# Hyena's filters and their spectra computed inside RWKV's preparation stage; the shift by a token as a product with a constant matrix

## The reference, cut to what matters

```python
# RWKV: mix with the two neighbours, per segment (256 context rows, 1024 latent rows)
x = u + mu * (0.5 * (u_before + u_behind) - u)        # zero beyond the ends of a segment
# then per token: kk = k * w_kk, normed per head; w, a = sigmoid(base + tanh(..) @ lora); k per direction

def hyena_filters(length, w1, b1, f1, w2, b2, f2, w3):
    ...
    hid = jnp.sin(f1 * (z @ w1 + b1))
    hid = jnp.sin(f2 * (hid @ w2 + b2))
    h = (hid @ w3).reshape(length, HY_ORDER, 2, HY_W)
    return (h * jnp.exp(-t * deltas)[:, None, None, :]).astype(F32)
# two_sided_fftconv multiplies the spectrum of the input by the spectrum of (h_f, h_b), for two orders
```

## Time and profile before

| | us |
|---|---|
| median of 3 runs (5839.44 to 5861.69) | 5848.86 |
| the profiled execution: time / span | 5849.2 / 5847.6 |
| PE busy in the span | 4508.9 (77%) |
| DVE busy | 2637.6 (45%) |
| ACT busy | 1397.6 (24%) |
| POOL busy | 650.7 (11%) |
| mean granted TensorE clock, share of full speed | 0.863 |

### The profile page before, as it was taken

One profiled execution on the slowest core, in us unless ns is written; L12 is line 12 of the kernel. 1 busy time (PEld: TensorE's weight loads), 2 busy tenths in 40 slices (PEclk: granted clock), 3 DMA queues, 4 the chain that ended last, 5 costly groups with the idle time before them and its releaser, 6 DMA issues. The chain is left out here.

```text
span 5847.6 us, 71599 instructions
## 1 busy us (share of the span) xinstructions
PE 4508.9 (77%) x26346; PEld 3697.1 (63%) x26346; DVE 2637.6 (45%) x4928; ACT 1397.6 (24%) x2564; POOL 650.7 (11%) x640
## 2 busy tenths in 40 slices
PE   6999987677998991899552169995489966876877
PEld 4998874455887881899552048885379952333555
DVE  3567743453332005211265766764533543323654
ACT  3233214432221002111022323332331100001333
POOL 1111111110000001000012221111112410110001
PEclk8999996688999995899865579997699976888998
DMA  4444422231112102221204543332434523343004
GB/s 153 161 143 139 136 97 104 83 112 58 47 47 61 54 18 102 92 96 56 90 23 164 197 123 99 99 95 66 133 118 131 190 95 137 140 156 121 7 7 151
DMA packets 433801, 599.74 MB, mean 103 GB/s; under 512 B 187209, under 2 KB 326065, under 8 KB 427331
## 3 DMA queue, kind: packets, MB, share of 16 engines
q1 hardware_dynamic: 377721, 443.54, 24.0%
q0 software_dynamic: 39824, 147.45, 6.5%
q10 hardware_dynamic: 16000, 5.30, 0.4%
HBM read 425.95 MB, written 170.25 MB: 102 GB/s over the span
## 5 line engine op out<-in xcount | busy, mean ns | idle before, releaser
L336 PE MATMUL g_in_g_acc<-g_in_g_whi,g_in_hi 128*128 128x444 f32 (+4 forms) x960 | 357.2, 372 | 15.2 <-DVE g_in_g_wlo L326 9.9
L337 PE MATMUL g_in_g_acc<-g_in_g_wlo,g_in_hi 128*128 128x444 f32 (+4 forms) x960 | 346.3, 361 | 0.0
L338 PE MATMUL g_in_g_acc<-g_in_g_whi,g_in_lo 128*128 128x444 f32 (+4 forms) x960 | 346.1, 360 | 0.0
L212 PE MATMUL g_even_acc<-g_even_w_hi,h_hi 128*128 128x384 f32 (+1 forms) x960 | 317.1, 330 | 30.6 <-DVE g_even_w_lo L254 30.6
L212 PE MATMUL g_down_acc<-g_down_w_buf,fT 128*128 128x256 f32 x1408 | 306.0, 381 | 16.5 <-DMA g_down_w_buf<-in_w_down 16.5
L214 PE MATMUL g_even_acc<-g_even_w_lo,h_hi 128*128 128x384 f32 (+1 forms) x960 | 316.9, 330 | 0.0
L215 PE MATMUL g_even_acc<-g_even_w_hi,h_lo 128*128 128x384 f32 (+1 forms) x960 | 316.9, 330 | 0.0
L212 PEld LDWEIGHTS g_down_acc<-g_down_w_buf,fT 128*128 128x128 f32 x1408 | 268.8, 191 | 53.7 <-DMA g_down_w_buf<-in_w_down 16.9
L336 PE MATMUL g_odd_g_acc<-g_odd_g_whi,h_hi 128*128 128x344 f32 (+3 forms) x816 | 262.9, 322 | 30.7 <-DVE g_odd_g_wlo L326 17.4
L338 PE MATMUL g_odd_g_acc<-g_odd_g_whi,h_lo 128*128 128x344 f32 (+3 forms) x816 | 261.1, 320 | 0.0
L337 PE MATMUL g_odd_g_acc<-g_odd_g_wlo,h_hi 128*128 128x344 f32 (+3 forms) x816 | 261.0, 320 | 0.0
(11 more groups left out here) (543 smaller groups left out, 10016.3 us busy)
## 6 DMA issues: line engine op xcount, KB each, us to landing
prep_x<-U2p SPq DMA_DIRECT2D x30, 896.0 KB, 5.6
g_in_m_w<-in_ada_w SPq DMA_DIRECT2D x24, 1024.0 KB, 5.7
up_w_buf<-in_w_up SPq DMA_DIRECT2D x44, 512.0 KB, 4.8
U2p<-g_even_o_buf POOLq DMA_DIRECT2D x11, 1920.0 KB, 7.8
g_odd_x<-U3p SPq DMA_DIRECT2D x24, 768.0 KB
g_even_w_buf<-in_even_w_in SPq DMA_DIRECT2D x11, 1536.0 KB
g_in_m_w<-in_w_ada SPq DMA_DIRECT2D x16, 1024.0 KB, 6.0
PD<-prep_od POOLq DMA_DIRECT2D x10, 1536.0 KB, 8.1
```

The lines of the kernel that those rows point to most:

```text
L212: mm = pe.matmul(o, hi[:, k, tt], w_hi[:, par, k, :wd], start=k == 0, stop=not split and k == kc - 1)
L336: pe.matmul(bank[:, :wd], hi[:, k, tt], w_hi[:, st % 2, k, :wd], start=k == 0, stop=False)
L337: pe.matmul(bank[:, :wd], hi[:, k, tt], w_lo[:, st % 2, k, :wd], start=False, stop=False)
L338: op = pe.matmul(bank[:, :wd], lo[:, k, tt], w_hi[:, st % 2, k, :wd], start=False, stop=k == KC - 1)
```

## The change

The stages `filter_stage` and `spectrum_stage` (twice) are gone. `rwkv_prep_stage` does their work beside its own. It has no loops any more: `order()` writes out one list of steps, and every engine walks the same list and issues its part of each step, in that order.

A tile t has four slots (4t to 4t+3). The 16 pieces of the filters (for each of eight tiles a `scale` and a `sum`) are spread over slots 0 to 11, i.e. tiles 0 to 2; the products of filter k+1 stand right behind `scale` k. Worked out from `share`: scale 0 to 7 fall into slots 0, 2, 3, 5, 6, 8, 9, 11. In slot 12 `z` of both orders and the first two chunks of `t_fwd` are loaded. The 16 units of the spectra are spread over slots 17 to 39: two in tile 4, two in tile 5, three in each of tiles 6 to 8 and three in tile 9. `spec_out` k-1 stands before unit k.

The shift: each tile is loaded once, and the two rows next to it by themselves (`outside`, two DMAs of one row). PE multiplies the tile by a constant 128x128 matrix with 0.5 beside the diagonal and -1 on it, and adds a product of the two outer rows with a 2x128 matrix, in four parts of 512, 512, 512 and 256 columns. The parts and the four low-rank products of a tile share a ring of three PSUM banks (`ring`, `freed`). DVE multiplies each part by mu and adds it to the tile. POOL and ACT have no part in the mix any more. `load_x(t + 2)` stands at the end of tile t.

```diff
-            def store(t, par, ahead):
-                ahead()
-                pool.wait_ge(s.k_done, t + 1)
...
+        def order():
+            yield "front", 0
+            yield "sine", 0
+            yield "sine", 1
+            yield "filter", 0
+            yield "shift", 0
+            yield "shift_out", 0
+            yield "mix", 0
+            yield "low", 0
+            yield "lora", 0
+            for t in range(NTA):
+                more = t + 1 < NTA
+                yield "norm", t
+                yield "slot", SLOTS * t
+                yield "okk", t
+                yield "lora_end", t
+                yield "lora_out", t
+                if more:
+                    yield "shift", t + 1
+                yield "slot", SLOTS * t + 1
+                yield "bonus", t
+                if more:
+                    yield "shift_out", t + 1
+                    yield "mix", t + 1
+                yield "slot", SLOTS * t + 2
+                if more:
+                    yield "low", t + 1
+                    yield "lora", t + 1
+                yield "dirs", t
+                yield "slot", SLOTS * t + 3
+                yield "dots", t
+            yield "spec_out", UNITS - 1
...
+            def load_x(t):
+                par = t % 2
+                if t >= 2:
+                    sp.wait_ge(s.k_done, t - 1)
+                    sp.wait_ge((s.rv_even, s.rv_odd)[par], t // 2 * (2 * DMA))
+                sp.dma_start(x[:, par], U2p[t * P + 1:(t + 1) * P + 1, U_SHIFT:EVEN_IN]).then_inc((s.x_even, s.x_odd)[par], DMA)
...
+                if what == "load_z":
+                    load_w(0)
+                    load_z(0)
+                    load_z(1)
+                    load_w(1)
...
+                if what == "filter":
+                    pe.wait_ge(s.sine, 2)
+                    if t:
+                        pe.wait_ge(s.scaled, t)
+                    for n in range(4):
+                        op = pe.matmul(acc[:, n], hid[:, t * P:(t + 1) * P], w3s[:, n * HYW:(n + 1) * HYW], start=True, stop=True)
+                    op.then_inc(s.w3_mm, 1)
...
+                    for n, (c, e) in enumerate(PARTS):
+                        use = 8 * t + n
+                        if use >= 3:
+                            pe.wait_ge(s.freed, use - 2)
+                        bank = ring[use % 3][:, 0:e - c]
+                        pe.matmul(bank, shift[:], x[:, t % 2, c:e], start=True, stop=False)
+                        pe.matmul(bank, ends2[:, kind], outside[:, c:e], start=False, stop=True).then_inc(s.ring, 1)
+                if what in ("lora", "lora_end"):
...
+                    for n, d in ((0, 0), (0, 1), (1, 0)) if what == "lora" else ((1, 1),):
+                        use, half = 8 * t + 4 + 2 * n + d, slice(d * 64, (d + 1) * 64)
+                        pe.wait_ge(s.freed, use - 2)
+                        pe.matmul(ring[use % 3][:], tT[half, n, :], lw[half, n, :], start=True, stop=True).then_inc(s.ring, 1)
...
+                if what == "shift_out":
...
+                        dve.tensor_tensor(diff[:, c:e], ring[use % 3][:, 0:e - c], mu_r[:, c:e], ALU.mult).then_inc(s.freed, 1)
+                if what == "mix":
+                    dve.drain()
+                    dve.tensor_tensor(x[:, par], x[:, par], diff[:], ALU.add)
...
-        filter_stage(nc, T["t_feats"], T["t_decay"], T["hy_w1_2"][0], T["hy_b1_2"][0], T["hy_f1_2"][0], T["hy_w2_2"][0], T["hy_b2_2"][0],
-                     T["hy_f2_2"][0], T["hy_w3_2"][0], FS)
         for order, (zin, zout) in enumerate(((VX[:, 0:HYW], Z1), (Z1, Z2))):
-            spectrum_stage(nc, f"spec{order}", T["t_fwd"], FS[order], KS[order])
```

More of the change, by code:

```diff
@@ L2093, in _, with shift_tables @@
             ahead(dve, decays, norm_gate)
[L2096 to L2112, removed]
+def shift_tables():
+    at = np.arange(P)
+    shift = 0.5 * (np.abs(at[:, None] - at[None, :]) == 1) - np.eye(P)
+    ends = np.zeros((2, 3, P), np.float32)
+    ends[0, 0:2, 0] = 0.5
+    ends[1, (0, 2), P - 1] = 0.5
+    return shift.astype(np.float32), ends
@@ new lines, in rwkv_prep_stage, with share, in_order @@
+def rwkv_prep_stage(nc, ident, U2p, mu, w0, w2, a0, a2, kk_w, ka, rk, t_shift, t_ends2, PC, PD, t_feats, t_decay, w1, b1, f1, w2h, b2, f2, w3, FS, t_fwd, KS):
+    SLOTS = 4
+    FILTER_SLOTS, SPEC_FROM = 3 * SLOTS, 4 * SLOTS + 1
+    UNITS = 2 * FCH * 2
+    SPEC_SLOTS = NTA * SLOTS - SPEC_FROM
+    PARTS = ((0, 512), (512, 1024), (1024, 1536), (1536, SHIFT_W))
+    def share(slot, slots, pieces):
+        return range(slot * pieces // slots, (slot + 1) * pieces // slots) if 0 <= slot < slots else ()
+    def order():
[30 more added lines that the diff above has]
+        yield "spec_out", UNITS - 1
+    def in_order(part):
+        for what, n in order():
+            if what != "slot":
+                part(what, n)
+                continue
+            for k in share(n, FILTER_SLOTS, 2 * NT):
+                part("sum" if k % 2 else "scale", k // 2)
+                if k % 2 == 0 and k // 2 + 1 < NT:
+                    part("filter", k // 2 + 1)
+            if n == FILTER_SLOTS:
+                part("load_z", 0)
+            for k in share(n - SPEC_FROM, SPEC_SLOTS, UNITS):
+                if k:
+                    part("spec_out", k - 1)
+                part("spec", k)
+    with stage(nc, "prep", "front", "const", "x_even", "x_odd", "outside", "mixed", "norm_sq", "root", "tanh", "turned", "tT",
+               "ring", "freed", "lora_b", "sig", "k_done", "rv_even", "rv_odd", "stored_even", "stored_odd",
+               "f_const", "f_cols", "h_mm", "arg", "sine", "dec_even", "dec_odd", "w3_mm", "scaled", "f_done", "fs0", "fs1",
+               "z0_in", "z1_in", "w_even", "w_odd", "s_mm", "odd_out", "s_out", "ks_even", "ks_odd") as (block, s, sb, ps):
+        x = sb("x", [P, 2, SHIFT_W])
+        outside = sb("outside", [2, SHIFT_W])
+        shift = sb("shift", [P, P])
+        ends2 = sb("ends2", [2, 3, P])
+        diff = sb("diff", [P, SHIFT_W])
+        mu_r = sb("mu_r", [P, SHIFT_W])
@@ L2126, in rwkv_prep_stage @@
         pt = ps("pt", [P, 2, P])
[L2127 to L2145, removed]
+        ring = [ps(f"ring{n}") for n in range(3)]
+        z = sb("z", [P, 2, 8 * SEQ])
+        feats, ang, turns, arg, hid = (z[0:64, 0, n * SEQ:(n + 1) * SEQ] for n in range(5))
+        w3s = z[0:64, 0, 5 * SEQ:7 * SEQ]
+        dec = z[:, 0, 7 * SEQ:8 * SEQ].rearrange("p (b c) -> p b c", b=2)
@@ L2151, in _ @@
[L2151 to L2181, removed]
@@ L2183, in _ @@
+            in_order(part)
             sp.wait_ge(s.rv_even, NTA // 2 * 2 * DMA)
@@ L2249, in _, with part @@
-            tiles(act, body, edge)
+            for n, v in enumerate((b1, f1, b2, f2)):
+                act.dma_start(cols[:, n:n + 1], v.rearrange("(p a) -> p a", a=1), allow_slow_non_contiguous=True).then_inc(s.f_cols, DMA)
+            def part(what, t):
+                par = t % 2
+                if what == "sine":
+                    act.wait_ge(s.arg, t + 1)
+                    act.activation(hid, arg, ACT.Sin).then_inc(s.sine, 1)
+                if what == "low":
+                    act.wait_ge(s.mixed, t + 1)
+                    if t:
+                        act.wait_ge(s.turned, t)
+                    act.activation(td[:, 0, :], x[:, par, 1536:1664], ACT.Tanh)
+                    act.activation(td[:, 1, :], x[:, par, 1664:1792], ACT.Copy)
+                    act.drain()
+                    act.sem_inc(s.tanh, 1)
+                    if t:
+                        act.wait_ge(s.ring, 8 * t)
+                    act.wait_ge(s.turned, t + 1)
+                    act.activation(tT[:], pt[:], ACT.Copy).then_inc(s.tT, 1)
+                if what == "norm":
+                    act.wait_ge(s.norm_sq, t + 1)
+                    act.activation(ss[:], ss[:], ACT.Sqrt).then_inc(s.root, 1)
+                if what == "lora_out":
+                    act.wait_ge(s.lora_b, t + 1)
+                    act.activation(sg[:], sg[:], ACT.Sigmoid).then_inc(s.sig, 1)
+                if what == "spec_out":
+                    act.wait_ge(s.s_mm, t + 1)
+                    if t >= 2:
+                        act.wait_ge(s.s_out, t - 1)
+                    act.activation(odd[:, par], acc[:, 2 * par + 1], ACT.Copy).then_inc(s.odd_out, 1)
```

447 lines of the change are left out of this document (223 added, 224 removed).

## The result

| | before | after |
|---|---|---|
| median, us (4 runs each) | 5855.27 | 5707.11 |
| lowest to highest | 5839.44 to 5875.34 | 5700.87 to 5711.66 |
| span of the profiled execution | 5847.6 | 5709.9 |

The ratio is 0.9744, with a 95% interval of 0.9711 to 0.9778: 2.6% faster. The forecast was 5692 us, 2.7% less.

The account below looks back on a forecast made before the run. Preparation was bound by DVE, filters and spectra by PE; in the new stage PE paces tiles 4 to 9. 56.5+154+199+7 = 416.5 us; 5849.2-573.8+416.5 = 5692 us, eight-in-ten range 5620 to 5775.

Parts of the forecast that it names:

- opening, to the first norm: New preparation's start: loads 8, layers 26.7, filter 0 7.2, shift 12.0, last part and addition 2.6; 56.5 us against 33.4 before.
- tiles 0 to 3: Preparation tiles with filter work, then the burst: 43.5, 38.9, 42.3 and 29.5 us, 154 in all, at 1.2 GHz.
- tiles 4 to 9, to DVE's last addition: Preparation tiles with spectrum units, PE setting the pace: terms sum to 201 us, the slot-by-slot walk gives 199.
- tail: From DVE's last addition to the next stage: taken as 7 us, between a spectrum's 6.4 and the preparation's 10.5.
- The price of the shift: PE's 14 MATMULs of 512 columns per tile: 12.0 us at half clock, 6.0 at full, 2-row products at full price.
- Clock: PE's clock in the new stage: 1.2 GHz in tiles 0 to 3, from tile 4 between half and full.
- Full clock: Rival, chance 0.22: PE stays at 2.4 GHz from tile 0, new stage 344 us, kernel 5619 us.
- half clock throughout: Rival, chance 0.12: the shift pulls PE's clock down, tiles 4 to 9 take 317 us, kernel 5810 us.
- The burst: SP's 10 MB of loads in slot 12, 28 us: units wait for nothing, x(5) at most 3 us later, taken as nothing.
- Turn by turn: Rival, chance 0.03: PE and DVE only alternate in the new stage, their times add to 737 us, kernel 6012 us.
- The change does little: Rival, chance 0.03: loads late behind the burst, each tile waits for DMA some 15 us, kernel 5842 us.
- the three signs of being wrong: In the new stage: clock 1.00 in tiles 0 to 3, short 2-row products (both faster), or DVE waiting for `x` (slower).

Follow-up runs that it names:

- shift_only_pad: The new preparation without filter and spectrum steps, old stages back, 2-row product padded with zeros to 128 rows: stage 261.6 us, median 5825.0 us, one run.
- pad_ends: Changed kernel with the product of the two outer rows padded with zeros to 128 rows: stage 394.7 us, median 5662.5 us, ratio 0.9670 to the kernel before.
- pad_both: pad_ends with the filters' products also padded with zeros from 64 to 128 rows: stage 384.8 us, median 5652.0 us, ratio 0.9657 to the kernel before.
- late_z: Changed kernel with the burst's second half issued behind tile 5's load: stage 411.0 us, median 5708.0 us, ratio 0.9746 to the kernel before.
- move_only: Changed kernel with the shift made by two more loads and DVE operations, not PE: stage 399.3 us, median 5672.2 us, ratio 0.9700 to the kernel before.
- shift_only: Changed kernel without filter and spectrum steps in the preparation, old stages back: stage 328.2 us, median 5895.6 us, ratio 1.0072 to the kernel before.

## Why the prediction was right, and where its sum was off

The forecast was 416.5 us of new stage. The profile has 441.6, and a second one of the same kernel (after_again) 424.4. By steps, with the first profile:

| step | forecast | measured |
|---|---|---|
| opening, to the first norm | 56.5 | 61.6 |
| tiles 0 to 3 | 154 | 161.8 |
| tiles 4 to 9, to DVE's last addition | 199 | 207.7 |
| tail | 7 | 10.6 |

- **The mechanism** is as forecast: PE's queue, with the shift in it, set the pace beside DVE's work. All three removed stages went whole, 292.7 us, and the rest behind them took the same 2159 us. The first convolution opened 1363.6 us after rwkv's first instruction, where the filter stage had opened after 1358.7.
- **The price of the shift** was the mis-sized term: 12.0 or 6.0 us, taken at full price for 2 rows. The 2-row product did cost as much as one of 128, but the two in turn cost 2.00 us a product, not 1.71: 14.3 and 7.6. That is 2.3 us in the opening and in each of tiles 0 to 3, 9 in these, where the sum missed 7.8. In after_again, with the same shift, tiles 0 to 3 took 149.5 us, less than the 154 forecast, as the clock was higher in two of them: a sum over these tiles is no finer than that. From tile 5's on the five shifts took 14.3, 10.5, 10.2, 7.6 and 8.3, 51 us where I had 45. The step left out that spectrum 0's rows, from which the price came, are of products all of one shape.
- **Clock**: 0.50 up to tile 3, as priced, then 0.62, 0.85 and 0.91. Full clock and half clock throughout are both out. The reason given (64-row and 2-row products and pauses in front of the units) is borne out in part: padding the rows raised the clock in shift_only_pad and in tile 1 of pad_ends and pad_both. Padding the 2-row product also hides its weight loads, and the two effects were not taken apart, nor was the part that pauses have.
- **The opening's loads** were put at 8 us; PE started at 3119.7, 10.9 from the start. With the shift's 2.3 that is the 5 missing in the opening.
- **The burst** was taken at nothing, with at most 3 us more; PE waited 8.0 us in tile 4, and late_z took it away. x(5) took 14.6 us from issue. The step counted the burst's 10 MB alone, issued at once 25 us earlier; it was issued from 3301.7 on, its last load only at 3316.5, 15.6 us ahead of x(5), and 17 MB moved from 3301.5 to 3346.7, with the stores and the tiles' own loads.
- **Tiles 4 to 9**: apart from that wait within 1 us of the walk, with PE nearly without gaps from the first unit on (34.05 of 34.90 us in tile 5). That closeness is luck in part: the shifts took 6 us more than priced, the units 122 where the walk had 125 and the low-rank products 18 where it had 23.
- **Tail**: 10.6, as long as the preparation's before and not the 6.4 of a spectrum. The last PD stores are issued 3.5 us ahead of the last KS store; what of the 10.6 is theirs was not tried.
- **Turn by turn** is out: 250 and 352 us of work in 442. **The change does little** is out: the kernel gained 148 us by the medians, and the DMA share is 0.41 over the stage. Of the three signs of being wrong one came in part: it was PE that waited for `x`, once, and not every tile.

The forecast did not ask what each half of the change is worth. It priced the shift at 12.0 us of the opening's +23 and as PE's load, and still took it as part of one gain; the runs say that the move gives 174 us and the shift takes some 30 back.

## What to carry to other kernels

Merging stages pays where one has the room that the other lacks, and two busy columns of one view show it: 293 us of filters and spectra made a preparation of 281 only 118 us longer (move_only). Price a new product from rows of the same neighbours, not only of the same size: in products of 128 and 2 rows in turn the first weight load of each was not hidden, and the clock stayed at 0.50 in shift_only. Zeros up to 128 rows took the same preparation from 47 us above the old one to 20 below it, most of these 20 in the opening. Count all that moves beside a burst of loads, not the burst alone. When two ideas come in one change, run each alone before the sum.

## What the runs showed of the hardware

- A MATMUL of 2 rows took as long as one of 128 (971 and 969 ns); alternating with it, each product of 512 columns took 1.05 us at full clock in place of 0.86, and 2.00 in place of 1.71 at half.
- A stage with PE busy 208 of 328 us was granted 0.50 throughout; the same stage with padded products, busy 136 of 261, was granted 0.66. Zeros in the filters' products, 64 rows more, went with 0.88 and 0.82 in tile 1 in place of 0.59.
- A load of 127 rows (889 KB) moved at 26 GB/s, and one of 128 rows (896 KB) landed in 5.6 us in the earlier trace rows. With 17 MB moving at 379 GB/s a load of 896 KB was in use only 14.6 us after its issue.
- The same code had a stage of 441.6 and of 424.4 us in two executions, by tiles at 0.50 or at 0.59 to 0.73, while the medians agreed within 2.3 us: where the clock swings so, 10 us of a stage are read from the tiles that an edit touches, or from the times of many executions.
